# Layer 2's scale span of the modulation, summed by GpSimd through layer 1 instead of multiplied by TensorE in layer 1's output projection

## The reference

```python
def adaln_params(cond, w_ada, b_ada):
    mod = jax.nn.silu(cond) @ w_ada + b_ada
    shift, scale, gate = jnp.split(mod, 3, axis=-1)
    return shift[:, None, :], scale[:, None, :], gate[:, None, :]
...
    shift, scale, gate = adaln_params(c, w_ada, b_ada)
    shift_c, scale_c, gate_c = adaln_params(c_ctx[None, :], w_ada, b_ada)
    h = rms_norm_2(x, norm_w) * (1 + scale) + shift
    hc = rms_norm_2(ctx, norm_w) * (1 + scale_c) + shift_c
    p = h @ w_in
    ...
    x_new = x + gate * merge_branches(p, o, lam_init, pool_w, pool_scale, subln_w, w_out)
```

## Time and profile before

| | us |
|---|---|
| median of 3 runs | 3003.23 (2996.53 to 3004.24) |
| the profiled execution | 3003.08 |
| its span, first to last instruction | 3001.3 |
| TensorE busy | 2852.5 |
| VectorE busy | 1910.9 |
| ScalarE busy | 1024.4 |
| GpSimd busy | 109.4 |
| mean granted clock of TensorE | 0.979 |

### The profile page before, as it was taken

One profiled execution on the slowest core, in us unless ns is written; L12 is line 12 of the kernel. 1 busy time (PEld: TensorE's weight loads), 2 busy tenths in 40 slices (PEclk: granted clock), 3 DMA queues, 4 the chain that ended last, 5 costly groups with the idle time before them and its releaser, 6 DMA issues.

```text
span 3001.3 us, 40313 instructions
## 1 busy us (share of the span) xinstructions
PE 2852.5 (95%) x16432; PEld 2350.3 (78%) x16432; DVE 1910.9 (64%) x2852; ACT 1024.4 (34%) x1515; POOL 109.4 (4%) x157
## 2 busy tenths in 40 slices
PE   6899999999998999999989999999999989999998
PEld 2588887786786888986877789767778877897888
DVE  3477677656887576455565577877576864538564
ACT  3223343225213233434332222334441232225463
POOL 0000000000000000000000000530000000004100
PEclk9999999999998999999999999999999989999999
DMA  9554344430555865434756755222534533322455
GB/s 404 233 175 163 122 153 143 159 116 36 180 199 178 288 228 183 160 114 143 275 189 234 265 212 183 104 91 106 181 120 156 182 111 123 97 92 91 151 180 169
DMA packets 145641, 501.90 MB, mean 167 GB/s; under 512 B 16048, under 2 KB 41392, under 8 KB 134960
## 3 DMA queue, kind: packets, MB, share of 16 engines
q1 hardware_dynamic: 136048, 489.65, 46.2%
q10 hardware_dynamic: 9408, 9.67, 0.9%
HBM read 484.05 MB, written 8.39 MB: 164 GB/s over the span
## 4 chain that ended last, share of the span: by engine, by line
PE 74%; DVE 8%; PEld 6%; issue 4%; DMA 3%; ACT 2%; POOL 1%; SPq 1%; PEldq 0%; DVEq 0%; ACTq 0%; POOLq 0%
PE products L1670 61%; PEld products L1670 5%; PE turned L1901 2%; DMA w_raw<-w_slots 2%; PE scores L1884 1%; DVE w_low L1076 1%; DVE tmp L1215 1%; PE modulation L1766 1%; ACT w_high L732 1%; DVE ada_w L1122 1%; PE products L1864 1%; DVE h_low L1243 1%; PEld turned L1901 1%; DMA mix_b<-ada_slots 1%; PE turned L1893 1%
## 5 line engine op out<-in xcount | busy, mean ns | idle before, releaser
L1670 PE MATMUL products<-h_high,w_high 128*128 128x512 f32 (+1 forms) x3424 | 1251.4, 365 | 84.3 <-DVE h_low L1243 33.0
L1670 PE MATMUL products<-h_low,w_high 128*128 128x512 f32 (+1 forms) x3424 | 1192.5, 348 | 0.0
L1670 PE MATMUL products<-h_high,w_low 128*128 128x512 f32 (+1 forms) x3424 | 1192.3, 348 | 0.0
L732 ACT CAST w_high<-w_raw 128x1024 fp32r<-128x1024 f32 x500 | 523.4, 1047 | 1327.0 <-PE products L1670 1135.9
L1076 DVE TENSOR_TENSOR w_low<-w_raw,w_high 128x1024 fp32r<-128x1024 f32 x500 | 614.5, 1230 | 557.5 <-ACT w_high L732 554.8
L1670 PEld LDWEIGHTS products<-h_high,w_high 128*128 128x128 f32 x3424 | 661.1, 193 | 254.7 <-issue 120.7
L1670 PEld LDWEIGHTS products<-h_low,w_high 128*128 128x128 f32 x3424 | 662.9, 194 | 79.4 <-issue 10.8
L1670 PEld LDWEIGHTS products<-h_high,w_low 128*128 128x128 f32 x3424 | 661.1, 193 | 81.1
L1122 DVE SCALAR_TENSOR_TENSOR ada_w<-ada_w,cond_silu 128x1024 f32<-128x1024 f32 x300 | 373.3, 1286 | 2.4 <-DMA ada_w<-mod_slots 0.7
L1670 PE MATMUL products<-w_high,h_high 128*128 128x256 f32 x640 | 183.3, 286 | 3.0 <-DVE w_low L1076 2.4
L1670 PE MATMUL products<-w_high,h_low 128*128 128x256 f32 x640 | 181.1, 283 | 0.0
(11 more groups left out here) (232 smaller groups left out, 2698.7 us busy)
## 6 DMA issues: line engine op xcount, KB each, us to landing
w_raw<-w_slots SPq DMA_DIRECT2D x500, 512.0 KB, 3.7
ada_w<-mod_slots SPq DMA_DIRECT2D x160, 512.0 KB, 3.7
ada_w<-ada_slots SPq DMA_DIRECT2D x58, 1024.0 KB, 7.8
mix_b<-gate_slots SPq DMA_DIRECT2D x32, 512.0 KB, 4.0
mix_a<-gate_slots SPq DMA_DIRECT2D x32, 512.0 KB, 4.2
mix_a<-ada_slots SPq DMA_DIRECT2D x12, 1024.0 KB, 14.3
mix_b<-ada_slots SPq DMA_DIRECT2D x10, 1024.0 KB, 15.1
x_scratch<-x_residual ACTq DMA_DIRECT2D x3, 2048.0 KB, 9.1
```

What stands on the lines that cost most here:

```text
L732: nc.scalar.copy(whi[:, n % SPL, :], raw[:, n % RAW, :]).then_inc(high_done, 1)
L1670: ins = nc.tensor.matmul(o, a, b, start=first and q == 0, stop=last and q == 2, skip_group_check=skip)
```

## The change

The scale span of layer 2 leaves the units. Its matrix is cut into 64 pieces of 256 KB (two column halves as blocks, in each 16 row tiles, in each two quarters). GpSimd loads each piece by a DMA of its own queue, multiplies it with both conditions (two TENSOR_SCALAR of 128x512) and adds both products to its sums (two TENSOR_TENSOR of 128x512; the first piece of a sum is written directly). The sums lie in the context half of `mix_a`, which layer 1 does not use; the pieces and products of the first block in `pool_values` and three tiles of `x_residual`, those of the second in `mix_b`, once the gate of layer 1 has been summed. GpSimd starts when layer 1's h is complete. TensorE sums each block with ONES after slots 173 and 233 (`QUIET_END`), and turns the row after slots 174 and 234.

```diff
-ADA_SPANS = ((2, 0), (2, 1), (2, 2))
+ADA_SPANS = ((2, 0), (2, 2))
...
+QUIET_SPAN = (2, 1)
+QUIET_PIECES = 2 * KC
+QUIET_END = {172: 0, 232: 1}
...
-        linear("out", layer, 4, toks, "feat", "res", "X", ada=4 if layer == 1 else 0, ahead=3,
+        linear("out", layer, 4, toks, "feat", "res", "X", ahead=3,
...
+        quiet_home = G[:, :, 0:S].rearrange("p (b t) n -> p b t n", t=2)
+        quiet_spare = pool_v[:, :, 0:S]
+        def quiet_w(block, half):
+            if block > 0:
+                return quiet_home[:, half, :, :]
+            return quiet_spare if half == 0 else xT[:, KC - 1, :].rearrange("p (t n) -> p t n", t=2)
+        def quiet_p(block, st):
+            if block > 0:
+                return quiet_home[:, 2 + st, :, :]
+            return xT[:, KC - 3 + st, :].rearrange("p (t n) -> p t n", t=2)
+        quiet_acc = Q[:, :, 0:S].rearrange("p (c h t) n -> p c h t n", c=2, h=2)
...
                                 if ph["layer"] > 0:
                                     sp.wait_ge(x_out, 16 * ph["layer"])
+                                    sp.wait_ge(quiet_added, 2 * (QUIET_PIECES - 2))
...
+            def quiet_load(p):
+                if p >= 2:
+                    pool.wait_ge(quiet_scaled, 2 * (p - 1))
+                if p == QUIET_PIECES:
+                    pool.wait_ge(gate_sum, 1)
+                nc.gpsimd.dma_start(quiet_w(p // QUIET_PIECES, p % 2), dram["quiet_slots"][p, :, :, :]).then_inc(quiet_landed[p % 2], 16)
+            def quiet_half(p):
+                b, chunk, h = p // QUIET_PIECES, p % QUIET_PIECES // 2, p % 2
+                cond = 2 * (QUIET_SPAN[0] // 2)
+                pool.wait_ge(quiet_landed[h], 16 * (p // 2 + 1))
+                if chunk == 0:
...
+                done = 2 * (p - 2 * (b + 1))
+                if done > 0:
+                    pool.wait_ge(quiet_added, done)
+                for st in range(2):
+                    c = sc32[:, chunk, cond + st:cond + st + 1]
+                    nc.gpsimd.tensor_scalar(quiet_p(b, st), quiet_w(b, h), c, None,
+                                            ALU.mult).then_inc(quiet_scaled, 1)
+                if p + 2 < 2 * QUIET_PIECES:
+                    quiet_load(p + 2)
+                for st in range(2):
+                    acc = quiet_acc[:, st, h, :, :]
+                    pool.wait_ge(quiet_scaled, 2 * p + st + 1)
+                    nc.gpsimd.tensor_tensor(acc, acc, quiet_p(b, st), ALU.add).then_inc(quiet_added, 1)
+            pool.wait_ge(cond_ready, 1)
+            pool.wait_ge(y_low, KC)
+            pool.wait_ge(x_out, 16)
+            pool.wait_ge(part_low, next(PARTS[pi] for pi, ph in enumerate(PH)
+                                        if ph["kind"] == "apply" and ph["layer"] == 1) + KC)
+            quiet_load(0)
+            quiet_load(1)
+            for p in range(2 * QUIET_PIECES):
+                quiet_half(p)
+            pool.wait_ge(quiet_scaled, 4 * QUIET_PIECES)
             step(nc.gpsimd.memset(pool_v[:, :, :], 0.0))
...
+            def quiet_sums(n):
+                if n - 1 not in QUIET_END:
+                    return
+                b = QUIET_END[n - 1]
+                pe.wait_ge(quiet_added, 2 * (QUIET_PIECES - 2) * (b + 1))
+                pe.wait_ge(*bank_free("quiet", b))
+                for j in range(4):
+                    ins = nc.tensor.matmul(AD[32 * j:32 * j + 32, :].rearrange("p (t n) -> p t n", t=2), ONES[:, 0:32],
+                                           quiet_acc[:, j // 2, j % 2, :, :], start=True, stop=True)
+                ins.then_inc(quiet_sum, 1)
```

More of the change, by code:

```diff
@@ L752, in block_row, with quiet_row @@
                 nc.scalar.copy(ada_row, AD[:, :]).then_inc(mod_rowed, 1)
+            def quiet_row(n):
+                if n - 2 not in QUIET_END:
+                    return
+                b = QUIET_END[n - 2]
+                act.wait_ge(*row_free("quiet", b))
+                act.wait_ge(quiet_sum, b + 1)
+                nc.scalar.copy(ada_row, AD[:, :]).then_inc(quiet_rowed, 1)
             def gate_row(n):
@@ L2264, in layout @@
         gate_slots=gates,
+        quiet_slots=quiet,
         x0=tiles(np.concatenate([i["ctx"][0], i["x"][0]])),
```

47 lines of the change are left out of this document (45 added, 2 removed).

## The result

The changed kernel takes 3051.8 us (median of 4 runs, 3041.2 to 3058.9), the kernel before beside it 3002.8: ratio 1.0165, 95% interval 1.0146 to 1.0184. The prediction was 3009 us with a range to 3028. The loss is 49 us, and it is outside the range. The profiled execution took 3041.2 us, so the trace shows some 38 us of it.

What follows compares the result with a forecast made beforehand. TensorE, busy 95% of the span, was taken as the bound, with VectorE under it in the output projection. 3003.1 - 6.6 (TensorE) + 9.7 (GpSimd beside VectorE) + 1.5 (loads) + 1.5 (clock) gave 3009 us, range 2995 to 3028.

Steps and rivals of the forecast that it cites:

- What bounds the kernel: Whole kernel: TensorE, busy 95% of the span; under it VectorE, twice in each output projection round of 8 slots.
- the third bullet (units as cover): Layer 1's output projection, rounds 1 to 3: removing each second pair of units gives back about 0.1 us, not 1.9.
- TensorE's balance, -6.6 us: Layer 1: 10.6 us saved by removing units and their products, less 4.0 us for the new ONES products and columns.
- GpSimd beside VectorE, +9.7 us: Layer 1 from 973 us: GpSimd's work lengthens VectorE's operations on the chain by 0.23 us each, 9.7 us in all.
- The 42 operations: VectorE operations on the chain beside GpSimd: 24 from 991.08 to 1308.54 us, two softmax scalings, 16 in the output projection.
- The signs named beforehand: Profile after: w_low between 973 and 1450 us averages 1.35 to 1.4 us; short steps around 1300 are 3 to 4 longer.
- Loads, +1.5 us: From 975 to 1010 us: GpSimd's 64 loads make three weight loads about a tenth longer, 1.5 us (0 to 5).
- The clock, +1.5 us: Output projection, rounds 1 to 3: one fall of the granted clock behind the new stalls, 1.5 us (0 to 4.5).
- Rival 1: Layer 1: units' cover and GpSimd's contention are both smaller than counted, giving 2994 us, or 2991 without contention; chance 0.15.
- Rival 2: Slot 173: TensorE waits for GpSimd's sums if a piece takes over 8.0 us; at 8.6, 3026 us; chance 0.22.
- Rival 3: VectorE's chain: each of 42 operations waits half a GpSimd instruction, 36 us instead of 9.7, giving 3035 us; chance 0.10.

Runs made afterwards that it cites:

- Neither: The changed kernel with GpSimd's arithmetic behind a sum's first piece cut to two of 512 columns, and loads behind a block's first two to a sixteenth: 3001.0 us, 0.9991.
- Run 6: The changed kernel with each of GpSimd's 128x512 operations cut into two of 128x256: 3082.5 us, 1.0276 of the kernel before.
- the multiplying run: The changed kernel with GpSimd's multiplications whole and its additions cut to two columns of 512: 3003.1 us, 1.0004 of the kernel before.

## Why the prediction was wrong

- **What bounds the kernel, and the third bullet (units as cover): right.** The stall in the middle of rounds 1 to 3 came as worked out, 1.74 us in each. What the output projection gave back, 5.4 us instead of some 8, fell short mostly in round 0, where GpSimd's last pieces still ran.
- **TensorE's balance, -6.6 us: right or somewhat too large.** "Neither" ended 7.5 us ahead in its trace, which was one of its faster executions; its median is 0.9991 of before, 3 us, with an interval from 6 us faster to 1 slower.
- **GpSimd beside VectorE, +9.7 us: this step failed.** The change with and without arithmetic differs by 1.0165 - 1.0012, 46 us. Two things were wrong in it. First the sentence "Elsewhere VectorE has room: in the other slots it works little over half of the time." This put the cost of those slots at nothing. Busy share is not slack. A slot's w_low cannot begin before ScalarE's w_high, and that not before the slot before last has been used, so of 2.92 us only 2.92 - 1.05 - 1.22 = 0.65 are free, and VectorE's 1.66 idle us lie ahead of the copy, where they help nobody. The 42 operations that I counted on the chain left out the w_low of every slot from 160 to 193. Second the price. From the earlier trace rows I took a mean excess of 0.23 us; from 1184 to 1411 us it is 1.94 - 1.22 = 0.72 us, and a mean of copies that lose nothing and of thirteen that lose 1.8 to 2.8 us. Against a slack of 0.65 us a mean of 0.23 is absorbed and such a single wait is not. The pooling could not have shown these waits: its 13 copies behind the earlier trace rows take 1.21 to 1.88 us, nine of them no more than 1.26, so even the longest loses 0.66 us. The rows below this list show why. The signs named beforehand were exceeded too: w_low from 973 to 1450 us averaged 1.80 us (of 83), not 1.35 to 1.4, and the short steps around 1300 us (slots 194 to 200) lost 9.9 us, not 3 to 4.
- **Loads, +1.5 us: too small.** Loads without arithmetic against neither: 1.0012 - 0.9991, 6 us (the two intervals just touch), all before slot 160, where the weights' loads are already on the chain.
- **The clock, +1.5 us: too small,** 11 us by its shares in one stretch, since there were many stalls instead of three.
- **Rival 1 (cover and contention smaller) did not happen:** the stalls came, and the contention was larger.
- **Rival 2 (TensorE waits for GpSimd): did not happen.** The 30 pieces from 987.1 to 1229.1 us took 8.1 us each instead of 7.5, which is just the point from which this rival decides (8.0), but TensorE was late itself and came 10 us behind GpSimd; that there was no wait is luck. The multiplications were mis-sized, 2.03 to 2.14 us instead of 1.71, the additions the other way, 1.39 instead of 1.65, and a load cost GpSimd 0.60 to 0.77 us and 0.30 of waiting. (At a piece of 8.15 us the rival's own formula gives a wait of some 3.5 us, not 5.) Run 6 shows the rival in full.
- **Rival 3 (the exclusion bites) was the nearest** and had a chance of 0.10. It priced 42 operations at 0.85 us, 36 us, against 46 measured; that the numbers are near is luck, since the places were not those and the single waits are of another size.

VectorE's copy that lost most in the pooling of the kernel before, and GpSimd's operations around it:

```profile
1913.84 1.88 DVE L1076 TENSOR_TENSOR w_low<-w_raw,w_high 128x1024 fp32r<-128x1024 f32 x1
...
1913.25 1.40 POOL L701 TENSOR_TENSOR pool_sums<-pool_values 128x528 f32<-128x528 f32 x1
1914.72 2.16 POOL L701 TENSOR_TENSOR pool_values<-pool_sums 128x512 f32<-128x512 f32 x1
```

There each of GpSimd's operations waits for the one before it, which leaves 0.08 us between the two: the copy ends 1.07 us behind the first and the second is the one that waits (2.16 us; one of its kind beside it took 1.27). In the changed kernel the two additions of a piece follow one another without a gap, and a copy stands through both. Whether a gap between them would save the second wait is not tested.

Three groups of GpSimd in the changed kernel (busy us, mean ns): the multiplications of the second block, the additions of the first, and half of the multiplications of the first:

```profile
L737 POOL TENSOR_SCALAR mix_b<-mix_b,cond_silu 128x512 f32<-128x512 f32 x60 | 116.2, 1942 | 5.1 <-POOL mix_a L744 5.0
L744 POOL TENSOR_TENSOR mix_a<-mix_a,x_residual 128x512 f32<-128x512 f32 x60 | 81.5, 1385 | 0.8
...
L737 POOL TENSOR_SCALAR x_residual<-x_residual,cond_silu 128x512 f32<-128x512 f32 x30 | 64.0, 2140 | 2.6 <-POOL mix_a L744 2.6
```

Two things stay open. The 4 us between "neither" (0.9991) and the expected balance (0.9978) are at the edge of its interval (from 0.9979). And of the stretch that is bound by loads (slots 122 to 160) the single traces differ by several us in runs of one kernel (the multiplying run was 2997.8 to 3011.8 us), so I don't split the lags there further.

## What to carry to other kernels

Before giving an idle engine work beside a busy one, ask for the slack of the copy that the bound engine waits for, from the event that releases it to the event that needs it, and not for its engine's busy share; then compare the longest single wait with that slack, not the mean, and take the wait from a stretch where the other engine issues the same operations in the same order: the pooling's longest was 0.66 us, that of the paired additions 2.8. Beside copies like these, GpSimd's multiplications by a column and its writes cost nothing that the runs resolve, and its additions nearly the whole loss; no run here leaves the multiplications to GpSimd and gives the additions to another engine. And work on the bound engine that stands in a stall is nearly free: moving six of its sixteen units by one slot gave more here (11 us) than taking all of them away (3 us).

## What the runs showed of the hardware

- A pair of GpSimd's TENSOR_TENSOR with both inputs in SBUF holds up VectorE's w_low to the end of the second: the copy of 1.22 us took 3.67 beside two additions of 2.53 together, up to 4.02 us, and ends 1.09 us behind the pair. Beside single additions with 0.08 us between them, in the pooling, it lost 0.66 us at most. By the trace's start times a copy that began up to 0.50 us ahead of the pair was held up as well, and one that began 0.71 us ahead or more was not. VectorE's w_low with one input was held up in the same way (3.76 against 0.69); its COPY from PSUM was not (1.23 us within a pair of additions). Whether it is the second input or the addition that makes the difference to TENSOR_SCALAR, no run separates.
- GpSimd's TENSOR_SCALAR (a multiplication by a column) holds up w_low by 0.48 us at most, and most copies not at all: 1.23 us in the median and 1.27 in the mean of 48, the longest 1.70. It waits itself: 1.55 us alone, up to 4.4 beside VectorE. MEMSET does not hold w_low up: 1.22 us with GpSimd busy 74 of 82 us.
- The Trainium skill (SBUF — State Buffer, Who interferes with whom) says that the shared port pair is an exclusive lock for the whole instruction: a VectorE operation in a two-port mode contends with GpSimd, and one with two SBUF inputs contends with a GpSimd operation that reads SBUF, not with one that only writes it. The additions and the writes agree with it in the traces, and the one-input copy does if it runs in such a mode, which no trace names. The multiplications read SBUF as well, and a copy that meets one ends 0.2 us behind it where the additions' ends 1.09 behind, so it does not wait for the whole instruction; here the measurement decides.
- A DMA issued by GpSimd takes 0.60 to 0.77 us of its time and a wait of 0.30 before it.
